# Attention values on TensorE: one fp32 product per tile replaced by three fp32r passes

## The reference

```
def one_block(args):                     # one block of 128 queries, all heads
    q_blk, k_blk, v_blk, blk_idx = args  # 32 query heads on 8 key/value heads, 64 wide
    s = einsum('bqkgd,bckd->bkgqc', q_blk, k_blk) * ATTN_SCALE
    s = where(valid, s, -inf)            # band: the own block and the one before
    m = maximum(max(s, axis=-1), sink)
    p = exp(s - m)
    w = p / (sum(p, axis=-1) + exp(sink - m))
    return einsum('bkgqc,bckd->bqkgd', w, v_blk)
```

## Time and profile before

| what | value |
|---|---|
| median of 3 runs | 2444.58 us (2444.52 to 2445.36) |
| profiled execution, its own time | 2443.17 us |
| its span, first to last instruction | 2441.4 us |
| mean granted TensorE clock | 0.998 |
| busy: TensorE matmul / weight load | 99% / 84% of the span |
| busy: VectorE / ScalarE / GpSimd | 67% / 47% / 3% |
| DMA | 446.18 MB, mean 183 GB/s |

### The profile page before, as it was taken

One profiled execution on the slowest core, in us unless ns is written; L12 is line 12 of the kernel. 1 busy time (PEld: TensorE's weight loads), 2 busy tenths in 40 slices (PEclk: granted clock), 3 DMA queues, 4 the chain that ended last, 5 costly groups with the idle time before them and its releaser, 6 DMA issues.

```text
span 2441.4 us, 33739 instructions
## 1 busy us (share of the span) xinstructions
PE 2418.1 (99%) x12352; PEld 2047.2 (84%) x12352; DVE 1632.3 (67%) x2181; ACT 1140.2 (47%) x1583; POOL 68.7 (3%) x83
## 2 busy tenths in 40 slices
PE   9999999999999999999999999999999999999998
PEld 8888888888888888888888888888888888888886
DVE  7888888886568556556556577775875664655655
ACT  5555555554345444445445354453643443443441
POOL 0100100000000000000000000000000000000000
PEclk9999999999999999999999999999999999999999
DMA  8655555546657666566566545336676666655653
GB/s 236 181 162 166 161 166 163 164 156 218 196 184 220 225 191 189 190 187 185 195 190 185 196 150 196 110 108 196 188 230 194 187 189 194 188 192 183 196 190 112
DMA packets 486486, 446.18 MB, mean 183 GB/s; under 512 B 13616, under 2 KB 359904, under 8 KB 485072
## 3 DMA queue, kind: packets, MB, share of 16 engines
q1 hardware_dynamic: 484608, 433.52, 58.8%
q0 software_dynamic: 1744, 10.81, 1.3%
HBM read 442.18 MB, written 2.10 MB: 182 GB/s over the span
## 4 chain that ended last, share of the span: by engine, by line
PE 94%; DVE 4%; DMA 1%; ACT 1%; issue 1%; POOL 0%; SPq 0%; DVEq 0%; ACTq 0%
PE ps L453 25%; PE ps L474 15%; PE ps L476 15%; PE ps L475 15%; PE ps L455 13%; PE ps L526 2%; PE ps L507 2%; PE ps L505 2%; PE ps L506 2%; PE ps L615 1%; DVE wlo L1290 1%; PE ps L758 1%; PE ps L736 1%; DMA raw<-in_a_w_in 1%; ACT whi L850 0%
## 5 line engine op out<-in xcount | busy, mean ns | idle before, releaser
L1290 DVE TENSOR_TENSOR wlo<-raw,whi 128x1024 fp32r<-128x1024 f32 x817 | 997.4, 1226 | 549.7 <-ACT whi L850 542.1
L850 ACT ACTIVATE whi<-raw 128x1024 fp32r<-128x1024 f32 x817 | 860.4, 1057 | 751.7 <-PE ps L476 509.4
L453 PE MATMUL ps<-actA,whi 128*128 128x512 f32 x2704 | 957.4, 399 | 1.3 <-issue 0.7
L455 PE MATMUL ps<-actA,wlo 128*128 128x256 f32 x2704 | 757.2, 280 | 0.7 <-issue 0.7
L453 PEld LDWEIGHTS ps<-actA,whi 128*128 128x128 f32 x2704 | 507.6, 188 | 126.9 <-issue 4.9
L455 PEld LDWEIGHTS ps<-actA,wlo 128*128 128x128 f32 x2704 | 510.3, 189 | 2.7 <-issue 1.7
L474 PE MATMUL ps<-whi,actB 128*128 128x512 f32 x1056 | 412.8, 391 | 0.1
L476 PE MATMUL ps<-whi,actB 128*128 128x512 f32 x1056 | 411.1, 389 | 0.0
L475 PE MATMUL ps<-wlo,actB 128*128 128x512 f32 x1056 | 411.0, 389 | 0.0
L476 PEld LDWEIGHTS ps<-whi,actB 128*128 128x128 f32 x1056 | 198.2, 188 | 41.5
L474 PEld LDWEIGHTS ps<-whi,actB 128*128 128x128 f32 x1056 | 198.3, 188 | 41.4 <-DVE actB L1302 0.5
(11 more groups left out here) (222 smaller groups left out, 1814.0 us busy)
## 6 DMA issues: line engine op xcount, KB each, us to landing
raw<-in_mlp_w SPq DMA_DIRECT2D x512, 512.0 KB, 4.1
raw<-in_a_w_in SPq DMA_DIRECT2D x162, 512.0 KB, 4.2
raw<-in_a_w_out SPq DMA_DIRECT2D x64, 512.0 KB, 4.3
raw<-in_b_w_q SPq DMA_DIRECT2D x32, 512.0 KB, 4.5
raw<-in_b_w_o SPq DMA_DIRECT2D x32, 512.0 KB, 3.7
raw<-in_kv_w SPq DMA_DIRECT2D x16, 512.0 KB, 3.5
gb<-in_ln_g POOLq DMA_DIRECT2D x4, 1024.0 KB, 7.0
gb<-in_ln_b POOLq DMA_DIRECT2D x4, 1024.0 KB, 9.3
```

The lines of the kernel that those rows point to most:

```text
L453: e.matmul(ps[:, b, :].rearrange("p (a n) -> p a n", a=2), whi[:, s, w], act[:, kt, :, :], start=(kt == 0), stop=False)
L455: last = e.matmul(ps[:, b, T:2 * T], wlo[:, s, w], act[:, kt, 0, :], start=False, stop=(kt == KT - 1))
L850: e.activation(whi[:, s, :], raw[:, r, :], ACT.Copy).then_inc(w_hi_done, C.up(w_hi_done))
L1290: e.tensor_tensor(wlo[:, s, :], raw[:, r, :], whi[:, s, :].bitcast(F32), ALU.subtract).then_inc(w_split, C.up(w_split))
```

## The change

V is written in two parts, `vtok[:, h, 0, :]` (rounded to fp32r) and `vtok[:, h, 1, :]` (the rest). The turned probabilities leave PSUM in two parts as well: ScalarE writes `p_hi` of each bank, then VectorE reads the bank again, subtracts `p_hi` and frees the bank. Each fp32 product of the values becomes three fp32r passes. `vtok` and `otok` move to space of constants of the first layer.

```diff
+    p_hi_done = nc.alloc_semaphore("p_hi_done")
+    v_hi_done = nc.alloc_semaphore("v_hi_done")
...
-    vtok = place("vtok", [P, NH, BLK], F32, sel_at)
+    vtok = place("vtok", [P, NH, 2, BLK], F32R, ssm_at)
+    otok = place("otok", [P, BLK], F32, ssm_at + 2 * NH * BLK * 4)
...
-    pT = put("pT", [P, 8, P])
+    pT = put("pT", [P, 2, 8, P], F32R)
     qT = put("qT", [P, 4, T])
-    otok = put("otok", [P, BLK])
...
                 fill(6)
+                v = slice(kv * HD, (kv + 1) * HD)
                 for i in range(4):
+                    o = ps[:, 6, i * HD:(i + 1) * HD]
                     for kc in range(1 + c):
-                        last = e.matmul(ps[:, 6, i * HD:(i + 1) * HD], pT[:, (1 + c) * i + kc, :],
-                                        vtok[:, kc, kv * HD:(kv + 1) * HD], start=(kc == 0), stop=(kc == c))
+                        p_hi, p_lo = pT[:, 0, (1 + c) * i + kc, :], pT[:, 1, (1 + c) * i + kc, :]
+                        e.matmul(o, p_hi, vtok[:, kc, 0, v], start=(kc == 0), stop=False)
+                        e.matmul(o, p_hi, vtok[:, kc, 1, v], start=False, stop=False)
+                        last = e.matmul(o, p_lo, vtok[:, kc, 0, v], start=False, stop=(kc == c))
                 last.then_inc(full[6], C.up(full[6]))
...
-            def pT_out(b):
+            def p_hi(b, k):
                 e.wait_ge(full[b], C.next(full[b]))
-                e.activation(pT[:, 0:4, :], tiles(b), ACT.Copy).then_inc(free[b], C.up(free[b]))
+                e.activation(pT[:, 0, k:k + 4, :], tiles(b), ACT.Copy).then_inc(p_hi_done, C.up(p_hi_done))
...
                 for u, (b, c, j) in enumerate(UNITS):
-                    pT_out(P_BANK[u])
+                    p_hi(P_BANK[u], 0)
                     if c:
-                        C.n[full[7]] += 1
+                        p_hi(7, 4)
                     step()
...
-            def pT_out():
-                e.wait_ge(full[7], C.next(full[7]))
-                e.tensor_copy(pT[:, 4:8, :], tiles(7)).then_inc(free[7], C.up(free[7]))
+            def p_lo(b, k):
+                e.wait_ge(p_hi_done, C.next(p_hi_done))
+                e.tensor_tensor(pT[:, 1, k:k + 4, :], tiles(b), pT[:, 0, k:k + 4, :].bitcast(F32), ALU.subtract).then_inc(
+                    free[b], C.up(free[b]))
+                C.n[full[b]] += 1
...
                     if turn:
                         q_rope(2 * ((b + 1) % 2), used[b + 1], (0,))
+                    p_lo(P_BANK[u], 0)
                     if c:
-                        pT_out()
-                    elif P_BANK[u] == 7:
-                        C.n[full[7]] += 1
-                        C.n[free[7]] += 1
+                        p_lo(7, 4)
...
                     for h in range(NH):
-                        e.tensor_copy(vtok[:, h, :], ps[:, 2 + h, :]).then_inc(free[2 + h], C.up(free[2 + h]))
+                        e.tensor_copy(vtok[:, h, 0, :], ps[:, 2 + h, :]).then_inc(v_hi_done, C.up(v_hi_done))
+                    for h in range(NH):
+                        e.wait_ge(v_hi_done, C.now(v_hi_done, back=1 - h))
+                        e.tensor_tensor(vtok[:, h, 1, :], ps[:, 2 + h, :], vtok[:, h, 0, :].bitcast(F32),
+                                        ALU.subtract).then_inc(free[2 + h], C.up(free[2 + h]))
```

More of the change, by code:

```diff
@@ L211, in build @@
     ident = place("ident", [P, P])
+    amask = place("amask", [P, 2, P])
+    lng = place("lng", [P, 4, KT])
+    lnb = place("lnb", [P, 4, KT])
+    ssm_at = at[0]
     tri = place("tri", [P, P])
-    amask = place("amask", [P, 2, P])
     csx = place("csx", [P, NH, 2, P], F32R)
@@ L216, in build @@
     selg = place("selg", [P, 4 * GH])
-    sel_at = at[0]
     csm = place("csm", [P, GH, P], F32R)
@@ L221, in build @@
     nw = place("nw", [P, DI // P])
-    lng = place("lng", [P, 4, KT])
-    lnb = place("lnb", [P, 4, KT])
     dt = place("dt", [P, NH, NHD])
@@ L227, in build @@
     Dsk = place("Dsk", [P, NHD])
+    assert at[0] - ssm_at >= (2 * NH + 1) * BLK * 4
     cosb = place("cosb", [P, NH, 32])
@@ L1899, in sums, with output @@
                 e.reciprocal(rinv, den).then_inc(dve_step, C.up(dve_step))
-            def output(b, c, j, p_bank):
-                e.wait_ge(full[6], C.next(full[6], 2 if p_bank == 6 else 1))
+            def output(b, c, j):
+                e.wait_ge(full[6], C.next(full[6]))
                 e.wait_ge(dve_step, C.now(dve_step))
@@ L1949, in attention @@
                         o_lo(u - 1)
-                    output(b, c, j, P_BANK[u])
+                    output(b, c, j)
                     if o_first and u and UNITS[u - 1][2]:
```

## The result

| | before | after |
|---|---|---|
| median | 2445.36 us (7 runs, 2442.52 to 2447.63) | 2455.04 us (7 runs, 2453.57 to 2459.84) |
| ratio | | 1.0042, 95% interval 1.003 to 1.0053 |
| profiled execution | 2443.17 us | 2456.68 us |
| its span | 2441.4 us | 2454.9 us |

The change makes the kernel 0.42% slower. The forecast was 2455.7 us, the range 2450 to 2460. In the last group of experiments one execution of the kernel before took 4048.64 us at a granted clock of 0.555, and it is left out of that group's ratios.

The account below looks back on a forecast made before the run. TensorE was taken to bound the kernel nearly everywhere. 10.4 us for 96 more pairs plus 0.8 us of waits made 11.2 us, added to the 2444.58 us median: forecast 2455.7 us, range 2450 to 2460.

Parts of the forecast that it names:

- price of a pair: At the values on TensorE, each load and matmul pair costs 0.108 us; 96 more pairs make 10.4 us more.
- (a): Recorded loads last 188 ns at L474 (fp32r) and 192 ns at L758 (fp32), against 140 ns for the transposes at L526.
- (b): Where TensorE comes out of the values, L475's fp32r load, waiting only for L474's, starts 0.11 us after it.
- rival by streamed columns: If fp32r loads hid fully at the values, a pair would cost 0.029 us: 2436.9 us in all; chance 0.08.
- middle price: Loads at the values as short as those of the transposes, 0.063 us a pair: 2445.1 us, no change; chance 0.08.
- VectorE's chain: In units 1, 5 and 9 `p_lo` adds 0.69 us, TensorE's own stream 0.43: 0.8 us more waiting in all.
- Units with c = 1: Second `p_lo` ends 0.7 us later; 3.2 us of slack hides the later maxima, and both are done before the values.
- Unit 12: TensorE's 0.90 us wait for `o_lo`: its chain moves 0.4 us, about what the values add; nothing extra.
- V's split: Two subtractions of 0.69 us after the `vtok` copies, 1.4 us of VectorE once; TensorE does not wait there: nothing.

Follow-up runs that it names:

- the kernel with V stationary: Changed kernel with V as stationary operand, 64 columns loaded, and 512 columns of turned probabilities streamed: median 2446.37 us, 1.0001 of the kernel before.
- the kernel with two passes: Changed kernel with all splits, `p_lo` written but its pass left out, 192 load and matmul pairs: median 2448.88 us, 1.0014 of the kernel before.
- one load of `p_hi`: Changed kernel with `p_hi` loaded once for both parts of V, VectorE adding the halves, 192 pairs: median 2454.38 us, 1.0033 of the kernel before.

## Why the prediction was right, point by point

- **The price of a pair** was taken as 0.108 us, from the fp32 loads' floor and one distance between two fp32r loads. Measured: 0.111 to 0.112 us, and it follows the loaded columns (0.058 at 64) and not the streamed ones (0.111 at 32 and at 128). Points (a) and (b) of the prediction held; the sum of 10.4 us for TensorE compares with 10.6 us more busy time, and with 96 x 0.111 = 10.7. The total is right in part by luck: this term was 0.3 us too low and that of the waits 0.4 too high, so that 11.2 met a stretch 11.0 us longer. (2444.58 + 11.2 is 2455.8, not the 2455.7 written.)
- **The rival by streamed columns** (2436.9 us) fell with these runs. The rule for small matmuls that stood behind it (the Trainium skill, "TensorE: Matmul & The Clock Gate", "Back-to-back issue gap") gives 25 ns for the gap of a single matmul of up to 64 columns; that isn't reached here, where each matmul has its own 128-column load. The load rule of the same page of the Trainium skill (columns divided by 1.2) comes near both measured prices: 107 and 53 ns by the rule, 111 to 112 and 58 measured.
- **The middle price**, 0.063 us, wasn't paid at the values. The transposes of the earlier trace rows that gave it load 128 columns too, of 48 rows, so 0.11 us is the price of these products' loads and not of every load of 128 columns. What makes those shorter was not tried.
- **VectorE's chain** in units 1, 5 and 9 was priced at +0.69 us each, so 0.26 of more waiting. It grew by 0.56, and the waits by 0.4 us in all, not 0.8. In unit 1 the mask operation after `p_lo` held the chain for 1.15 us in place of 1.24. VectorE's busy time in the stretch grew by 9.7 us and not by 11.3, as two `p_lo` in a row overlap: 1.26 us for both, below. Timeline after (against the earlier trace rows):

```profile
1528.73 0.69 DVE L1856 TENSOR_TENSOR ropeA<-ps,cosb 128x512 f32<-128x512 f32 x1 [0.50 <-PE ps L479]
...
1530.93 0.68 DVE L1918 TENSOR_TENSOR pT<-ps,pT 128x512 fp32r<-128x512 f32 x1
...
1537.73 0.42 DVE L1911 TENSOR_TENSOR otok<-ps,small 128x256 f32<-128x256 f32 x1
...
1538.29 1.06 PE L529 MATMUL ps<-ident,pb 128*128 128x128 f32 x8 [0.60 <-DVE otok L1911]
```

- **Units with c = 1** behaved as said: the later maxima are hidden, in unit 3 both `p_lo` are done by 1553.5 us (against the earlier trace rows) and the values start at 1554.97:

```profile
1552.26 1.26 DVE L1918 TENSOR_TENSOR pT<-ps,pT 128x512 fp32r<-128x512 f32 x2
...
1553.43 0.69 DVE L1891 TENSOR_TENSOR ps<-ps,amask 128x512 f32<-128x512 f32 x1
...
1554.97 0.19 PE L764 MATMUL ps<-vtok,pT 128*128 128x64 f32 x1
```

- **Unit 12** (against the earlier trace rows): the wait went from 0.90 to 0.82 us, nothing extra, as forecast. **V's split** shows nowhere in TensorE's waits.
- **What I had wrong** showed only in the experiments. With TensorE's work cut back, VectorE's chain costs more than the three times 0.56 or 0.69 us that I gave it: it reaches back into the units before. And a long wait can cost more than itself: after one of 2.63 us the clock took another 1.7. Even the kernel with V stationary, whose 72 matmuls hold TensorE for 4 us less than the fp32 products did (72 x 0.23 = 16.6 us against 20.6), brought no gain over the kernel before. So the 2436.9 us that I gave the rival by streamed columns were probably too low as well.

## What to carry to other kernels

Count load and matmul pairs before counting columns: with 128 stationary columns in 4 bytes a pair at the values costs 0.11 us whether it streams 32, 64 or 128 columns, so three fp32r passes in place of the two pairs of fp32 are half as dear again for a product 64 columns wide. At 512 columns they would be a fifth cheaper, by an estimate from the earlier trace rows: 3 x 0.23 = 0.69 us against 2 x 4 x 0.108 = 0.86; no run here has an fp32 product that wide. If a split has to be made there, load the narrow operand and stream the wide one, or let one load serve both parts of the other operand; here neither was faster than the kernel before, and the run with V stationary left the output in the wrong order. And price an operation added on a helper engine at each place where the main engine waits for it, back through the units before: the waits grew by 0.4 us beside passes that covered the rest, and the stretch by 2.7 us without them.

## What the runs showed of the hardware that I had not expected

- The MLP's row tiles, alternating 512 and 256 columns with the weights stationary, run at different paces in the same kernel, mostly 0.347 or 0.353 us a pair (0.356 in one slab of the kernel with two passes), for the length of a slab of some 256 pairs and at a granted clock of 1.00; the times step by 1.4 or 2.4 us. What selects the pace was not tried.
- Two loads in a row of the same stationary tile cost as much as two different ones (192 ns each, 0.11 us apart).
- The granted clock fell to 0.50 for 3.4 us after one idle time of 2.63 us of TensorE, and not after another of the same length in the same kernel (one load of `p_hi`).
- A 64-column load of `p_hi` (fp32r) is recorded with 138 ns, near the 140 ns of the transposes' loads of 128 columns in the earlier trace rows.
